# Latent attention: sums of squares of seven heads as two rounded passes in place of plain float

## The reference, cut to what matters

```
MLA_HEADS = 8; MLA_NOPE = 128; MLA_ROPE = 64; N_META = 16      # L = 512 + 16 = 528 keys, 512 queries used
def _rmsnorm(x, w):
    xf = x.astype(jnp.float32)
    y = xf * lax.rsqrt(jnp.mean(xf * xf, axis=-1, keepdims=True) + EPS)
    return (y * w.astype(jnp.float32)).astype(x.dtype)
...
    q = (_rmsnorm(q_lat, q_lat_w) @ w_uq).reshape(B, L, MLA_HEADS, MLA_NOPE + MLA_ROPE)
    kv = (_rmsnorm(kv_lat, kv_lat_w) @ w_ukv).reshape(B, L, MLA_HEADS, MLA_NOPE + MLA_V)
    q_nope, q_pe = q[..., :MLA_NOPE], q[..., MLA_NOPE:]
    k_nope, v = kv[..., :MLA_NOPE], kv[..., MLA_NOPE:]
    q_nope = _rmsnorm(q_nope, qn_w)
    k_nope = _rmsnorm(k_nope, kn_w)
    q_pe = _rope(_rmsnorm(q_pe, qpe_w), ...)
    # per head: softmax((q_nope k_nope^T + q_pe k_pe^T) * scale) @ v, then times silu(g)
```

## Time and profile before

| | us |
|---|---|
| median of 3 runs (1283.19 to 1284.58) | 1283.66 |
| the profiled execution, its own time | 1283.79 |
| its span in the profile | 1282.0 |
| TensorE busy | 1262.3 |
| GpSimd busy | 625.9 |
| VectorE busy | 714.1 |
| ScalarE busy | 468.9 |

### The profile page before, as it was taken

The page is one execution under the profiler, slowest core; times in us unless marked ns, Lnnn a source line. Parts: engine busy times, 40 slices in busy tenths (PEclk is TensorE's granted clock), DMA queues, the critical chain, the costliest instruction groups (busy, mean ns, idle before and its releaser), DMA issues.

```text
span 1282.0 us, 19992 instructions
## 1 busy us (share of the span) xinstructions
PE 1262.3 (98%) x6790; PEld 1036.4 (81%) x6790; DVE 714.1 (56%) x1379; ACT 468.9 (37%) x1017; POOL 625.9 (49%) x416
## 2 busy tenths in 40 slices
PE   7999999999999999999999999999999999999998
PEld 6877777877788888888888888888888888888876
DVE  5236665566865445442324788778643666666641
ACT  4232343412322222221113466666402555555431
POOL 5423333247353444445564154444347877777622
PEclk9999999999999999999999999999999999999999
DMA  6322222223233323323333211111133322222213
GB/s 201 103 51 82 82 75 72 67 83 100 81 115 98 98 84 96 98 78 103 94 103 99 67 50 51 50 33 49 49 97 95 95 79 78 78 78 78 65 34 99
DMA packets 190611, 105.42 MB, mean 82 GB/s; under 512 B 19174, under 2 KB 186444, under 8 KB 190556
## 3 DMA queue, kind: packets, MB, share of 16 engines
q1 hardware_dynamic: 189748, 102.82, 28.3%
q10 hardware_dynamic: 376, 1.18, 0.2%
q0 software_dynamic: 432, 0.69, 0.2%
HBM read 102.57 MB, written 2.10 MB: 82 GB/s over the span
## 4 chain that ended last, share of the span: by engine, by line
PE 90%; DVE 5%; ACT 2%; issue 1%; DMA 1%; POOL 1%; ACTq 0%; DVEq 0%
PE ps L391 20%; PE ps L392 20%; PE ps L393 20%; PE ps L422 9%; PE ps L1452 1%; PE ps L1534 1%; PE ps L1536 1%; PE ps L1535 1%; PE ps L1463 1%; PE ps L1483 1%; PE ps L1207 1%; PE ps L404 1%; PE ps L405 1%; PE ps L408 1%; DMA x_tok<-in_x_dram 1%
## 5 line engine op out<-in xcount | busy, mean ns | idle before, releaser
L370 POOL TENSOR_TENSOR w_low<-w_raw,w_high 128x1024 fp32r<-128x1024 f32 x180 | 440.6, 2450 | 465.0 <-DVE w_high L365 459.8
L391 PE MATMUL ps<-h_high,w_high 128*128 128x512 f32 x810 | 327.6, 404 | 0.5 <-DVE h_low L531 0.4
L392 PE MATMUL ps<-h_low,w_high 128*128 128x512 f32 x810 | 319.9, 395 | 0.0
L393 PE MATMUL ps<-h_high,w_low 128*128 128x512 f32 x810 | 318.8, 394 | 0.0
L365 DVE CAST w_high<-w_raw 128x1024 fp32r<-128x1024 f32 x183 | 150.0, 821 | 115.4 <-DMA w_raw<-in_w_in_dram 35.5
L391 PEld LDWEIGHTS ps<-h_high,w_high 128*128 128x128 f32 x810 | 152.2, 188 | 38.3 <-issue 3.8
L393 PEld LDWEIGHTS ps<-h_high,w_low 128*128 128x128 f32 x810 | 152.3, 188 | 34.7
L392 PEld LDWEIGHTS ps<-h_low,w_high 128*128 128x128 f32 x810 | 152.1, 188 | 33.8 <-issue 2.4
L1787 ACT ACTIVATE z<-ps,cv 128x512 f32<-128x512 f32 x42 | 32.7, 778 | 147.1 <-PE ps L393 147.1
L2404 DVE SCALAR_TENSOR_TENSOR z<-ps,cv,z 128x511 f32<-128x511 f32 x42 | 31.5, 749 | 90.5 <-ACT z L1787 90.5
L392 PE MATMUL ps<-m_low,w_high 128*128 128x512 f32 x176 | 69.4, 395 | 0.0
(11 more groups left out here) (388 smaller groups left out, 2402.4 us busy)
## 6 DMA issues: line engine op xcount, KB each, us to landing
w_raw<-in_w_in_dram SPq DMA_DIRECT2D x150, 256.0 KB, 3.2
w_raw<-in_w_up_dram SPq DMA_DIRECT2D x88, 256.0 KB, 3.2
w_raw<-in_w_out_dram SPq DMA_DIRECT2D x44, 256.0 KB, 3.0
w_raw<-in_w_down_dram SPq DMA_DIRECT2D x32, 256.0 KB, 3.0
w_raw<-in_w_down_dram SPq DMA_DIRECT2D x16, 192.0 KB, 2.6
rel<-in_rel_bias_dram SPq DMA_DIRECT2D x16, 192.0 KB, 3.6
w_raw<-in_w_ob_dram SPq DMA_DIRECT2D x8, 256.0 KB, 2.9
w_raw<-in_w_oa_dram SPq DMA_DIRECT2D x8, 256.0 KB, 4.2
```

Of the source, the lines that this page charges most:

```text
L370: pool.tensor_tensor(w_low[:, n % RING, :], w_raw[:, n % RAW, :], w_high[:, n % RING, :].bitcast(F32), ALU.subtract).then_inc(low_made, 1)
L391: pe.matmul(acc, wh, mh, start=first and k == 0, stop=False)
L392: pe.matmul(acc, wh, ml, start=False, stop=False)
L393: done = pe.matmul(acc, wl, mh, start=False, stop=last and k == tiles - 1)
```

## The change

The sums of all items of heads 1 to 7 that are marked below now take rounded parts: item 1 of heads 1 to 7, item 0 of heads 2, 4 and 6, item 2 of heads 1, 3, 5 and 7. ScalarE squares the value a second time into a rounded tile (`square_parts`: the not yet used `kn_high`, or slice 6 of `y_high`), GpSimd subtracts this from the plain square (`m_square_low`), and TensorE adds both parts in two passes with `ones_r` or `blocks_r`. Head 0, and item 2 of even heads, stay plain. For odd heads item 2's sum moves behind the first part of the gate product (for head 1: behind the scores of quarter 2). `ones_r` is one more small copy, and some semaphores are merged to free names (`ws_cut`, `pe_sum`), with the order of waits unchanged.

```diff
+        def square_parts(c, item):
+            if item == 1:
+                return kn_high[:, c % 2, :], kn_low[:, c % 2, :]
+            return y_high[:, 6, :], y_low[:, 6, :]
...
 # GpSimd, in m_squares, for item in range(c % 2, 2):
                     pool.tensor_tensor(dst, src, src, ALU.mult).then_inc(s["p_sq01"], 1)
+                    if c:
+                        pool.wait_ge(s["p_sq01"], i * 3 + (heads(c, 2, 1) + nth(c, item) + 1))
+                        m_square_low(i, c, item)
+                if c % 2:
+                    pool.wait_ge(s["p_sq2"], i * 2 + (c + 1))
+                    m_square_low(i, c, 2)
+
+            def m_square_low(i, c, item):
+                pool.wait_ge(s["p_sq_high"], i * 4 + (2 * c - 2 + nth(c, item) + 1))
+                hi, lo = square_parts(c, item)
+                src = sq[:, 1, :] if item == 1 else sq[:, 0, 0:S]
+                pool.tensor_tensor(lo, src, hi.bitcast(F32), ALU.subtract).then_inc(s["p_sq_low"], 1)
...
 # TensorE, in m_sums:
+                if c and (item < 2 or c % 2):
+                    pe.wait_ge(s["p_sq_low"], i * 4 + (2 * c - 2 + nth(c, item) + 1))
+                    if item == 2:
+                        pe.wait_ge(s["p_kept2"], i * 2 + (c + 1))
+                    for n, part in enumerate(square_parts(c, item)):
+                        if item == 1:
+                            for b in range(2):
+                                mm = pe.matmul(ps[:, 2 + b, 0:HALF], ones_r[:], part[:, b * HALF:(b + 1) * HALF],
+                                               start=n == 0, stop=n == 1)
+                        else:
+                            mm = pe.matmul(ps[:, 7, :], ones_r[:] if item else blocks_r[:], part, start=n == 0, stop=n == 1)
+                    mm.then_inc(s["p_sum"], 1)
+                    return
...
 # TensorE, in head_then_odd:
                 m_sums(i, c + 1, 1)
-                m_sums(i, c + 1, 2)
                 if c:
                     m_gate(i, c + 1, 0)
+                    m_sums(i, c + 1, 2)
                 m_scores(i, c, 2)
+                if c == 0:
+                    m_sums(i, c + 1, 2)
...
 # ScalarE, in m_keep, and the new m_square_high:
                 act.activation(dst, src, ACT.Copy).then_inc(s["p_kept01"], 1)
+                if c:
+                    hi = square_parts(c, item)[0]
+                    act.activation(halves(hi) if item else hi, src, ACT.Square).then_inc(s["p_sq_high"], 1)
+            def m_square_high(i, c):
+                act.wait_ge(s["p_kept2"], i * 2 + (c + 1))
+                act.activation(square_parts(c, 2)[0], q_f[:], ACT.Square).then_inc(s["p_sq_high"], 1)
...
 # ScalarE, in head_then_odd:
                 m_square(i, c + 1)
                 if c:
                     m_sigmoid(i, c)
+                m_square_high(i, c + 1)
+                if c:
                     y_rounded(i, c - 1)
```

More of the change, by code:

```diff
@@ L99, in program @@
         blocks_r = sb("blocks_r", [P, P], F32R)
+        ones_r = sb("ones_r", [P, P], F32R)
         cv = sb("cv", [P, C_V + V_ROWS])
@@ L433, in program @@
         names = """consts_in more_in ident_in x_in x_rest_in meta_in ones_set in_turned x_ready cols_ready gain_ready
-            meta_ready ws_cut ws_made
+            meta_ready ws_made
             norm_sq norm_sum norm_added norm_root norm_scaled norm_high norm_low
@@ L442, in program @@
             z_first z_mid z_done z_silu z_gated z_high z_low d_added d_placed
-            raw_high raw_low raw_used raw_kept lat_sq lat_sum lat_root lat_scaled lat_high lat_low pe_root_part pe_sum
+            raw_high raw_low raw_used raw_kept lat_sq lat_sum lat_root lat_scaled lat_high lat_low pe_root_part
             pe_part pe_turned tables_in
-            pe_split twice_in p_made p_kept01 p_sq01 p_sq2 p_kept2 p_sum p_root p_normed x_high x_low xp_low qr_turned qr_part
+            pe_split twice_in p_made p_kept01 p_sq01 p_sq_high p_sq_low p_sq2 p_kept2 p_sum p_root p_normed x_high x_low xp_low qr_turned qr_part
             mv_cleared mv_kept mv_turned mv_high_ mv_low_ mg_part mg_done
@@ L670, in _ @@
                     pool.affine_select(out=ws_raw[:], in_=ws_raw[:], compare_op=ALU.is_ge, fill=0.0, base=0,
-                                       pattern=[[0, 8], [-1, P]], channel_multiplier=1).then_inc(s["ws_cut"], 1)
+                                       pattern=[[0, 8], [-1, P]], channel_multiplier=1).then_inc(s["ws_made"], 1)
             for n0, n1 in ((N_GATE, N_MERGE), (N_MERGE, N_OUT)):
@@ L919, in _ @@
                 if n == 5:
-                    pe.wait_ge(s["ws_cut"], 1)
+                    pe.wait_ge(s["ws_made"], 1)
                     pe.wait_ge(s["gain_ready"], 2)
@@ L962, in _ @@
                 elif m == 2:
-                    pe.wait_ge(s["ws_made"], 2)
+                    pe.wait_ge(s["ws_made"], 3)
                 elif m == 4:
@@ L1168, in kpe_sums @@
                                    start=True, stop=True)
-                mm.then_inc(s["pe_sum"], 1)
+                mm.then_inc(s["pe_turned"], 1)
             def kpe_turn():
@@ L1258, in m_sums @@
                     return
+                if c and (item < 2 or c % 2):
[11 more added lines that the diff above has]
+                    return
                 if item < 2:
-                    pe.wait_ge(s["p_sq01"], i * 3 + (heads(c, 2, 1) + nth(c, item) + 1))
+                    pe.wait_ge(s["p_sq01"], item + 1)
                 else:
@@ L1271, in m_sums @@
                                        start=True, stop=True)
+                else:
+                    mm = pe.matmul(ps[:, 7, :], ones[:] if item else blocks[:], sq[:, 0, 0:S], start=True, stop=True)
                 mm.then_inc(s["p_sum"], 1)
@@ L1678, in _ @@
                 act.activation(sq[:, k % 2, 0:S], uv[:, 4 + k, :], ACT.Square).then_inc(s["sv_sq"], 1)
-            act.wait_ge(s["ws_made"], 1)
+            act.wait_ge(s["ws_made"], 2)
             act.activation(ws_t[:].rearrange("p (b g) i -> p b (g i)", b=2), ps[:, 6:8, :], ACT.Copy)\
@@ L1754, in _ @@
             act.activation(blocks_r[:], blocks[:], ACT.Copy)
+            act.activation(ones_r[:], ones[:], ACT.Copy)
             after(act, "att")
@@ L2000, in _ @@
             m_square(0, 0)
-            act.wait_ge(s["pe_sum"], 1)
+            act.wait_ge(s["pe_turned"], 1)
             act.activation(halves(kpe_root), wide(0), ACT.Ln, bias=eps[:, 0:1], scale=1.0 / 64)\
@@ L2663, in _ @@
             m_normed(0, 0, 2)
-            dve.wait_ge(s["pe_turned"], 1)
+            dve.wait_ge(s["pe_turned"], 2)
             dve.tensor_tensor(kpe_sq[:, 0:META], ps[:, 0, 0:META], sin[:, 0:META], ALU.mult)
```

## The result

| | before | after |
|---|---|---|
| median of 6 runs each, us | 1284.12 | 1288.06 |
| lowest to highest | 1282.9 to 1286.06 | 1287.6 to 1289.82 |
| ratio to before, 95% interval | | 1.0034 [1.0023, 1.0046] |
| profiled execution, its span | 1283.79, 1282.0 | 1288.06, 1286.3 |

The change makes the kernel 3.9 us slower by the medians; the ratio says 0.34%, and its interval reaches from 3.0 to 5.9 us. 6.0 were forecast, with the median at 1289.7 in a range of 1281.3 to 1292.3.

A forecast was written before the change was run, and what follows sets the result against it. The prediction took GpSimd locking VectorE out of the shared port, with TensorE waiting for VectorE, as the bound. Even heads 3.3, odd heads 1.2 and head 1 1.5 made 6.0 us more: 1289.7, range 1281.3 to 1292.3.

The forecast's parts named there:

- What bounds the kernel: Loop over heads: GpSimd's added operations hold VectorE's SBUF operations through the shared port, and TensorE waits for VectorE.
- TensorE's saving: Sums on TensorE: rounded matmuls take 5.5 us less work, 0.40 or 0.39 for each of 14 sums.
- Next head even: Three times: late low part of the `q_pe` squares, then `me` held behind `w_low`; +1.1 us each, bounds +0.2 and +1.4.
- Next head odd: Three times in the loop: `y_low` later, delaying `me`, `q_f` and `mp_low`; +0.4 us each, bounds 0 and +0.5.
- Head 1: Once: GpSimd's strip 2.6 us later behind two subtractions, holding `me` and `q_f`; +1.5 us, bounds 0 and +2.
- ScalarE: 14 added squares of about 0.5 us fit its gaps; costed at nothing except where they release GpSimd.
- The sum: Whole kernel: 3.3 for even heads, 1.2 for odd and 1.5 for head 1 make 6.0 us more, 1289.7.
- even heads at +0.2: Lower bound for each head where the next is even, if `me` slips in ahead of `w_low`.
- the saving arrives: Rival, 12%: subtractions fit GpSimd's idle time, VectorE is not held; 1278.2 us in full, 1281 with half lost.
- Gains and waits cancel: Rival, 20%: `q_pe` sum late but `me` not held by moved strips; even heads +0.3, odd nothing; 1284.6 us.

The follow-up runs named there:

- side work only: Changed kernel with squares and subtractions made but unused, TensorE adding plain squares in the old places: 1289.59 us against 1284.29 for the kernel before.
- split and order: Kernel before with GpSimd's low parts reordered, sums split only for item 1 (even heads), items 1 and 2 (odd), head 1 plain: 1279.17 against 1283.39 us.

## Why the prediction was right, point by point

*What bounds the kernel.* Right, and shown from both sides. Taking the subtractions away takes the loss away; making them without using them keeps 3.8 of 5.2 us. That operations which read PSUM are not held has its number too: before, `mp_low` takes 0.69 us all 32 times, 23 of them started while a GpSimd operation was under way. By the page "SBUF — State Buffer" of the Trainium skill, section "SBUF: two separate sides", the port is held for whole instructions. The trace agrees: the `me` of 2.40 us ends 0.28 us behind the strip's low part.

*TensorE's saving.* Its busy time fell by 4.4 us, for 5.5 forecast from the pace of the matmuls. It reached the end in none of the heads, as forecast. In the odd heads of the loop the forecast was that the saving buys nothing, and without the subtraction it bought 0.03 us.

*Next head even.* +1.01 us each, for +1.1. The steps came in the forecast order, the low part first behind VectorE's cast (769.97 to 771.30), then `q_pe` behind the output's low part, then `me` behind the strip: it ends 9.97 us after GpSimd's first square starts (769.60 to 779.57), 10.14 by the forecast (866.36 to 876.5). The wait at the sum was 0.88 in the profile for 1.1: the low part ended 1.12 us behind the cast's end, where I had put its full 1.3.

*Next head odd.* +0.29 for +0.4. The scaling of `me` lasted 0.75 where 0.89 were forecast: GpSimd's pair stood 0.1 us earlier than `y_low` had, 4.32 us after the start of the keys' copy (795.91 to 800.23) for 4.42 or 4.43.

*Head 1.* +1.51 for +1.5. The strip and the scaling stand where they were put (1.99 us for `me`). I had not priced the moved queries' sum, which costs 0.49 when it is plain and alone. The 1.5 does not need it: with the side work only, and that sum in its old place, head 1 costs 1.51 too.

*ScalarE.* Nothing was the forecast for its squares, and in the changed kernel nothing shows. Without the subtraction, though, ScalarE's root is what VectorE waits for in even heads, 0.50 us. The reason given, that it has gaps of that size, does not hold there.

*The sum.* A turn of the loop takes 50.1 us (768.82 to 818.90 between two copies of `q_pe`), for 50.3. The stage is 5.2 us longer for 6.0, the largest part of the difference in the three even and three odd heads at 0.1 each. The run time grew by 3.9 to 4.3, and its interval ends just short of the 6.0. So the mechanism is confirmed to 0.1 us a head, and the total is somewhat too high. In the profiled execution of the changed kernel the stage begins 0.7 us sooner (734.7 for 735.4) ahead of all changed sums. Over the nine profiles that start lies between 734.7 and 738.9, so 0.7 is within the spread. One bound of the prediction is off by its own terms: with even heads at +0.2 the sum is 3.3, so 1287.0 and not 1286.5.

*The rivals.* That the saving arrives was wrong for this order of work, and right for another: in the run with split and order 3.0 of 3.6 us arrive. "Gains and waits cancel" had as its condition that `me` is not held. The rows show it held in all seven: by the strip in head 1 and the even heads, where it was held before too but ended sooner, and by the output's low part in the three others.

## What to carry to other kernels

When work moves off the busiest engine, price the place where it lands by what it stands in front of, not by that engine's idle share: GpSimd was idle half of the time and the 18 us put on it cost 5. Two engines that lock each other out for whole instructions must be read as one list, in order of time. Then the cheap remedy is order. The same 14 subtractions, in the same place, cost 5.2 us when the output's and the strip's low parts follow them at once. When these two, which nobody needs so soon, are held back until VectorE has done the operations that TensorE waits for, the change costs nothing against the kernel before, and 0.5 us against the same order without it. And ask who is next in line: without the subtractions it was ScalarE.

## What the runs showed of the hardware

- An operation that waits on GpSimd for the one before it starts 0.16 to 0.17 us after that one's end (770.91 and 773.61 in the changed kernel), while operations that wait for nothing follow with no gap (774.90). I had put both at nothing.
- A one-input operation is locked out like a two-input one: the scaling of `me`, 512 columns from SBUF to SBUF. The page "VectorE: DVE Perf Modes" of the Trainium skill, section "Mode 2×_2P — use both read ports for one tensor", says that such an operation uses both read ports of VectorE to run twice as fast, and that one with an operand in PSUM cannot. The times fit: 0.49 us here against 0.69 for a copy of as many columns out of PSUM (0.70 at 880.40 in the earlier trace rows), and 0.69 for a cast of twice as many from SBUF to SBUF when it is free. No run shows the mode itself.
- A hold can be several times the held operation: 2.40 us for one that takes 0.49, when it is asked for 0.25 us after GpSimd's longest one has begun. By the readings above it would have gone first if asked for before that; no run has such a request at this place.
